# First adaLN rows of layer 0: shifts on TensorE into one PSUM bank, scales as row products on the vector engine, another load order; and another tile order in the first W2 block of an MLP chunk

## The reference

```
sh1, sc1, g1, sh2, sc2, g2 = split(silu(cond) @ mod_w[i] + mod_b[i], 6)
h = rmsnorm(x, norm1_g[i]) * (1 + sc1) + sh1
x = x + g1 * mixer_i(h)              # layer 0: gated short convolution; layer 1: latent attention
h = rmsnorm(x, norm2_g[i]) * (1 + sc2) + sh2
x = x + g2 * (square(relu(h @ mlp_w1[i])) @ mlp_w2[i])      # d_ff = 4096
```

## Time and profile before

| | |
|---|---|
| median of 3 runs | 3317.0 us (3314.32 to 3317.49) |
| profiled execution | 3313.17 us, span 3311.3 us |
| mean granted TensorE clock | 0.954 |
| PE busy | 3070.7 us (93%) |
| DVE busy | 1469.5 us (44%) |
| ACT busy | 1011.1 us (31%) |
| POOL busy | 855.9 us (26%) |
| chain that ended last | PE 61%, issue 23%, DVE 9%, ACT 4%, POOL 2% |

### The profile page before, as it was taken

One profiled execution on the slowest core, in us unless ns is written; L12 is line 12 of the kernel. 1 busy time (PEld: TensorE's weight loads), 2 busy tenths in 40 slices (PEclk: granted clock), 3 DMA queues, 4 the chain that ended last, 5 costly groups with the idle time before them and its releaser, 6 DMA issues.

```text
span 3311.3 us, 43718 instructions
## 1 busy us (share of the span) xinstructions
PE 3070.7 (93%) x17193; PEld 2931.1 (89%) x17193; DVE 1469.5 (44%) x1856; ACT 1011.1 (31%) x1447; POOL 855.9 (26%) x509
## 2 busy tenths in 40 slices
PE   7999998999999999877888888888898999999999
PEld 7999998999999999876777777776798999999999
DVE  2654545555544556554455554564324222222222
ACT  2211113111111112223666667556613111111111
POOL 0122111212212121111553446445421112212121
PEclk6999998999999999886999999899999999999999
DMA  4122220222111221200000000000110111111111
GB/s 192 66 84 94 75 90 32 77 77 82 63 69 64 89 76 63 93 11 7 6 7 2 7 5 7 8 6 0 77 44 26 45 39 44 44 38 39 44 44 76
DMA packets 45532, 166.60 MB, mean 50 GB/s; under 512 B 5792, under 2 KB 7456, under 8 KB 45216
## 3 DMA queue, kind: packets, MB, share of 16 engines
q1 hardware_dynamic: 44912, 160.89, 13.9%
q10 hardware_dynamic: 560, 4.87, 0.4%
HBM read 156.15 MB, written 9.58 MB: 50 GB/s over the span
## 4 chain that ended last, share of the span: by engine, by line
PE 61%; issue 23%; DVE 9%; ACT 4%; POOL 2%; DVEq 0%; ACTq 0%; POOLq 0%
PE ps L822 58%; PE ps L1068 2%; POOL w_lo L459 2%; DVE sums L1586 2%; DVE row_max L1568 1%; ACT p L745 1%; DVE hid_lo L1306 1%; DVE tmp L1301 1%; PE ps L1054 1%; ACT hid_hi L594 1%; ACT tmp L591 1%; DVE q_tok L1543 1%; DVE ssq L1508 0%; DVE k_tok L1548 0%; DVE x L1272 0%
## 5 line engine op out<-in xcount | busy, mean ns | idle before, releaser
L459 POOL TENSOR_TENSOR w_lo<-w_raw,w_hi 128x1024 fp32r<-128x1024 f32 (+2 forms) x190 | 463.4, 2439 | 1979.0 <-ACT w_hi L532 1979.0
L822 PE MATMUL ps<-h_hi,w_hi 128*128 128x384 f32 x2640 | 607.7, 338 | 49.5 <-DVE h_lo L1253 24.6
L822 PE MATMUL ps<-h_lo,w_hi 128*128 128x384 f32 x2640 | 604.2, 336 | 0.0
L822 PE MATMUL ps<-h_hi,w_lo 128*128 128x384 f32 x2640 | 603.1, 336 | 0.0
L822 PEld LDWEIGHTS ps<-h_hi,w_hi 128*128 128x128 f32 x2640 | 474.6, 190 | 54.0 <-issue 43.7
L475 POOL TENSOR_TENSOR p_lo<-p,p_hi 128x512 fp32r<-128x512 f32 (+1 forms) x304 | 384.2, 1273 | 433.8 <-ACT p_hi L747 429.8
L532 ACT ACTIVATE w_hi<-w_raw 128x1024 fp32r<-128x1024 f32 (+2 forms) x190 | 194.6, 1025 | 984.1 <-PE ps L822 912.1
L822 PEld LDWEIGHTS ps<-h_lo,w_hi 128*128 128x128 f32 x2640 | 475.4, 190 | 0.0
L822 PEld LDWEIGHTS ps<-h_hi,w_lo 128*128 128x128 f32 x2640 | 474.2, 189 | 0.0
L1272 DVE SCALAR_TENSOR_TENSOR x<-ps,mod,x 128x256 f32<-128x256 f32 (+5 forms) x432 | 240.1, 611 | 480.0 <-PE ps L822 478.3
L822 PE MATMUL ps<-hid_hi,w_hi 128*128 128x384 f32 x1536 | 350.4, 335 | 9.7 <-DVE hid_lo L1306 9.6
(11 more groups left out here) (135 smaller groups left out, 3587.3 us busy)
## 6 DMA issues: line engine op xcount, KB each, us to landing
w_raw<-in_wall_dram SPq DMA_DIRECT2D x174, 512.0 KB, 3.7
mod_raw<-in_mod_rows_dram SPq DMA_DIRECT2D x80, 512.0 KB, 3.5
mod_first<-in_mod_cols_dram SPq DMA_DIRECT2D x16, 512.0 KB, 15.2
x<-in_x_t_dram SPq DMA_DIRECT2D x8, 576.0 KB, 7.6
x_spill<-x ACTq DMA_DIRECT2D x1, 4608.0 KB, 15.2
x<-x_spill SPq DMA_DIRECT2D x1, 4608.0 KB, 13.7
out_dram<-x SPq DMA_DIRECT2D x8, 576.0 KB, 2.8
w_raw<-in_wall_dram SPq DMA_DIRECT2D x8, 416.0 KB, 3.1
```

The costliest lines, as they stand in the source:

```text
L459: pool.tensor_tensor(w_lo[s][:, 0:words], w_raw[s][:, 0:words], w_hi[s][:, 0:words].bitcast(F32), ALU.subtract).then_inc(w_lo_done, 1)
L822: ins = pe.matmul(out, lhs[a], rhs[b](cols), start=first and n == 0, stop=last and n == 2)
```

## The change

The first eight scales leave TensorE. SP loads their rows of the transposed `mod_w` (`scale_rows`, eight tiles of 512 KB, as many bytes as before) and the DVE makes each as two products against `cond_row` (`first_gain`), and the gain from it in one instruction more. TensorE keeps the eight shifts; they go side by side into 16 columns of bank 6 without a wait between them, three ahead of the sum of squares and five behind it, and one instruction adds all their biases (`shifts_out`). The inverse root stands behind the first two gains in the DVE's queue. ACT squares two tiles ahead of its copy of the condition rows, and makes its first two weight splits ahead of the root. `mod_bias` is loaded ahead of x; the shift tiles are interleaved with x, the first two weight blocks come next, and then scale and remaining shift tiles. In the MLP, the first W2 block of each chunk takes its tiles in an order written out by hand: three of the first half, two of the second, the fourth of the first, and the last two of the second.

```
+FIRST_SHIFTS, FIRST_GAINS = 3, 2
+DOWN_ORDER = [(0, 0), (0, 1), (0, 2), (1, 0), (1, 1), (0, 3), (1, 2), (1, 3)]
...
+        scale_bias = new("scale_bias", [P, KT])
-        mod_first0 = at("mod_first0", [P, KT, WSLOT], F32, G0)
+        mod_shift = at("mod_shift", [P, KT, WSLOT], F32, G0)
+        mod_junk = at("mod_junk", [P, WSLOT], F32, G0 + KT * WSLOT * 4)
-        mod_first1 = at("mod_first1", [P, KT, WSLOT], F32, H0 + KT * N * 4)
+        mod_scale = at("mod_scale", [P, KT, WSLOT], F32, H0 + KT * N * 4 + WSLOT * 4)
+        shift_ps = ps[:, 6 * BANK:6 * BANK + 2 * KT]
...
-            for j in range(KT):
+            sp.dma_start(mod_bias[:, :], T["mod_bias"]).then_inc(const_in, 16)
+            def load_x(j):
                 sp.dma_start(x[:, j, :], T["x_t"][:, j, :]).then_inc(x_loaded[j], 16)
-            sp.dma_start(mod_bias[:, :], T["mod_bias"]).then_inc(const_in, 16)
-            for m in range(FIRST_MODS):
-                tile = (mod_first0, mod_first1)[m // KT]
-                sp.dma_start(tile[:, m % KT, :], T["mod_cols"][m]).then_inc(mf_loaded[m], 16)
+            def load_shift(k):
+                sp.dma_start(mod_shift[:, k, :], T["mod_cols"][k]).then_inc(shift_loaded[k], 16)
+            def load_scale(k):
+                sp.dma_start(mod_scale[:, k, :], T["scale_rows"][k]).then_inc(scale_loaded[k], 16)
+            for j in range(0, KT, 2):
+                load_x(j)
+                load_x(j + 1)
+                load_shift(j // 2)
+            load(0)
+            load(1)
+            for k in range(KT // 2):
+                load_scale(k)
+                load_shift(KT // 2 + k)
+            for k in range(KT // 2, KT):
+                load_scale(k)
-            load_in(0, 0)
+            load_mod(0)
+            load_mod(1)
+            load(2)
+            load_mod(2)
...
-            act.wait_ge(row_mm, 1)
-            act.activation(cond_row[:, :, :].rearrange("p c n -> p (c n)"), ps[:, 0:2 * D], ACT.Copy).then_inc(row_out, 1)
-            rms(x_tile, KT, D)
+            for j in range(KT):
+                if j == 2:
+                    act.wait_ge(row_mm, 1)
+                    act.activation(cond_row[:, :, :].rearrange("p c n -> p (c n)"), ps[:, 0:2 * D],
+                                   ACT.Copy).then_inc(row_out, 1)
+                act.wait_ge(x_loaded[j], 16)
+                square(x[:, j, :], j % 2, D)
             split_hi()
             split_hi()
+            rms(None, 0, D)
+            act.wait_ge(mod_done, FIRST_MODS)
             norm(0, 0, False)
...
-            def first_mod(m):
-                b = 6 + m % 2
-                raw = (mod_first0, mod_first1)[m // KT][:, m % KT, :]
-                pe.wait_ge(mf_loaded[m], 16)
-                if m >= 2:
-                    pe.wait_ge(mod_done, m - 1)
+            def first_shift(k):
+                pe.wait_ge(shift_loaded[k], 16)
+                for j in range(KT):
+                    ins = pe.matmul(shift_ps[:, 2 * k:2 * k + 2], mod_shift[:, k, j * P:(j + 1) * P], cond[:, j, :],
+                                    start=j == 0, stop=j == KT - 1)
                 ins.then_inc(mod_mm, 1)
...
+            def first_down_block():
+                weights()
+                slot = L.at["b"] % 2
+                for half, t in DOWN_ORDER:
+                    if t == 0:
+                        pe.wait_ge(stage_free, L.count("s", 1 - half))
+                    if half == 0:
+                        pe.wait_ge(hid_lo_done, L.count("hid", -t - 1))
+                    v = stage_ps(L.at["s"] + half)
+                    w = t * 2 * P + half * P
+                    ins = three([(v[:, c, :], c) for c in range(3)], t, t == 0, t == HT - 1,
+                                [w_hi[slot][:, w:w + P], w_lo[slot][:, w:w + P]],
+                                [lambda c, h=h: h[:, t, c * TB:(c + 1) * TB] for h in (hid_hi, hid_lo)])
+                    if t == HT - 1:
+                        ins.then_inc(stage_done, 1)
+                L.at["s"] += 2
+                L.at["b"] += 1
...
-            for m in range(KT):
-                first_mod(m)
+            for k in range(FIRST_SHIFTS):
+                first_shift(k)
             pe.wait_ge(row_out, 1)
             sum_squares(KT)
-            for m in range(KT, FIRST_MODS):
-                first_mod(m)
+            for k in range(FIRST_SHIFTS, KT):
+                first_shift(k)
...
+            def shifts_out():
+                dve.wait_ge(mod_mm, KT)
+                dve.tensor_tensor(mod[:, 0:KT, :], shift_ps.rearrange("p (k c) -> p k c", c=2),
+                                  mod_bias[:, 0:KT].unsqueeze(2).to_broadcast([P, KT, 2]), ALU.add).then_inc(mod_done, KT)
+                L.at["m"] += KT
+            def first_gain(k):
+                dve.wait_ge(scale_loaded[k], 16)
+                raw, slot = mod_scale[:, k, :], k % 2
+                for c, product in enumerate((mod_junk[:, :], raw)):
+                    ins = dve.tensor_tensor_reduce(product, raw, cond_row[:, c, :], 1.0, 0.0, ALU.mult, ALU.add,
+                                                   mod_acc[:, slot, c:c + 1])
+                own(ins)
+                g0 = VEC["norm1_g"][0]
+                dve.tensor_scalar(gain[:, 0, k, :], mod_acc[:, slot, :], scale_bias[:, k:k + 1],
+                                  vec[:, g0 + k:g0 + k + 1], ALU.add, ALU.mult).then_inc(mod_done, 1)
+                L.at["m"] += 1
+                dve.wait_ge(mod_done, L.at["m"])
+            def first_norm():
...
+                own(dve.tensor_scalar(scale_bias[:, :], mod_bias[:, KT:2 * KT], 1.0, None, ALU.add))
+                dve.wait_ge(row_out, 1)
+                for k in range(KT):
+                    if k == FIRST_GAINS:
+                        inverse_root(False)
+                    first_gain(k)
+                dve.wait_ge(stage_free, L.at["s"])
+                scaled(0)
+                shifts_out()
+                for k in range(KT):
+                    if k + 1 < KT:
+                        scaled(k + 1)
...
-                first_mod_out(j)
-            inverse_root()
-            for m in range(KT, FIRST_MODS):
-                first_mod_out(m)
-            norm(0, 0, False)
+            first_norm()
```

More of the change, by code:

```diff
@@ L285, in build @@
         m_loaded = [sem(f"m_loaded{s}") for s in range(2)]
-        mf_loaded = [sem(f"mf_loaded{s}") for s in range(FIRST_MODS)]
+        shift_loaded = [sem(f"shift_loaded{k}") for k in range(KT)]
+        scale_loaded = [sem(f"scale_loaded{k}") for k in range(KT)]
         x_loaded = [sem(f"x_loaded{j}") for j in range(KT)]
@@ L930, in chunk @@
                             h_block()
+                    elif k == HT:
+                        first_down_block()
                     else:
@@ L933, in chunk @@
                         for half in range(2):
-                            def hid_ready(t):
-                                pe.wait_ge(hid_lo_done, L.count("hid", -t - 1))
-                            stage(lambda t: t * 2 * P + half * P, HT, (hid_hi, hid_lo),
-                                  hid_ready if k == HT and half == 0 else None)
+                            stage(lambda t: t * 2 * P + half * P, HT, (hid_hi, hid_lo))
                         L.at["b"] += 1
@@ L1174, in own @@
                 dve.wait_ge(dve_self, S.count("n"))
-            def first_mod_out(m):
-                dve.wait_ge(mod_mm, m + 1)
-                dve.tensor_scalar(mod[:, m, :], bank(6 + m % 2, 2), mod_bias[:, m:m + 1], None,
-                                  ALU.add).then_inc(mod_done, 1)
-                L.at["m"] += 1
+            def shifts_out():
[3 more added lines that the diff above has]
+                L.at["m"] += KT
@@ new lines, in first_norm, with scaled @@
+            def first_norm():
+                def scaled(k):
+                    if C["h"]:
+                        dve.wait_ge(h_lo_done, C["h"])
+                    for a, z, c in SEGS:
+                        ins = dve.scalar_tensor_tensor(tmp[k % 2][:, a:z], x[:, k, a:z], gain[:, 0, k, c:c + 1],
+                                                       rstd[:, a:z], ALU.mult, ALU.mult)
+                    ins.then_inc(t_done, 1)
+                    C["t"] += 1
+                own(dve.tensor_scalar(scale_bias[:, :], mod_bias[:, KT:2 * KT], 1.0, None, ALU.add))
[10 more added lines that the diff above has]
+                        scaled(k + 1)
+                    C["h"] += 1
+                    dve.wait_ge(t_done, C["t"] - (1 if k + 1 < KT else 0))
+                    dve.wait_ge(h_hi_done, C["h"])
+                    for a, z, c in SEGS:
+                        ins = dve.scalar_tensor_tensor(h_lo[:, k, a:z], tmp[k % 2][:, a:z],
+                                                       mod[:, k, c:c + 1], h_hi[:, k, a:z].bitcast(F32),
+                                                       ALU.add, ALU.subtract)
+                    ins.then_inc(h_lo_done, 1)
@@ L1214, in add_square, with inverse_root @@
```

(8 more changed lines are left out.)

4 lines of the change are left out of this document (removed).

## The result

The changed kernel took 3271.4 us (median of 4 runs, 3267.2 to 3273.1), the kernel before 3315.7 (median of 4, one run more than in the table above, which gave 3317.0); the ratio is 0.9867 with a 95% interval of 0.9850 to 0.9884. The forecast was 3275, range 3267 to 3288. The profiled execution took 3271.89 us, its span is 3270.1, 41.2 less than before.

The account below looks back on a forecast made before the run. TensorE was taken as the bound, with waits at the start and for hid_lo in each MLP chunk. Savings of 28.2 + 13.9 = 42.1 us took 3313.17 to 3271.1; 3.8 for median over profiled run gave 3275, range 3267 to 3288.

Parts of the forecast that it names:

- without the hold-up everything is 3.1 earlier: Start: bound if GpSimd's weight splits do not slow the DVE's products for the gains; 31.3 us saved.
- six gains, 18.0: Start: the DVE's remaining six gains behind the reciprocal take 18.0 us, ending at 52.5.
- 57.8: Start: forecast time in us of the first layer matmul, 85.97 before, so 28.2 saved.
- So the DVE decides, by about 1.3 us.: End of the start: the DVE's gains, first scaled tile and shift addition end at 54.4, TensorE's five shifts at 52.8.
- with all five shifts at the lower level: Start: bound where TensorE's shifts behind the broadcast all run at 1.2 GHz, end at 55.5 and decide; 26.9 us saved.
- the row behind the old broadcast: Start: earlier profile row with two shifts at the upper clock level (4.02 us) after the same broadcast; basis for 28.2 saved.
- 16 x 0.87: MLP: the wait for hid_lo goes whole in all 16 chunks of both layers, 0.87 us each, 13.9 us.
- The margin of 0.5 us for the residual: W2 blocks, layer 0: the DVE's residual ends at 587.8, TensorE wants that PSUM at 588.4.
- rival (a): W2 blocks: the wait returns as a wait for the residual; 3282 us, or 3289 if layer 1 gains nothing; chance 0.08.
- rival (c): Start: GpSimd does not hold up the DVE's products; 3272 us; chance 0.07.
- Rival (b): Start: saves much less because scale tiles and the reciprocal come late; 3277 to 3289 us, taken as 3285; chance 0.12.
- (d): Behind the start: TensorE stays at the lower clock level; four weight blocks cost 50 us, giving 3325; chance 0.02.

Follow-up runs that it names:

- e5_late_splits: Changed kernel with ScalarE's first two weight splits, and so GpSimd's, moved behind the last gain and shift; one run, 3269.5 us.
- e8_all: Changed kernel with early weight blocks and splits, four shifts ahead, one W2 tile between, additions of squares behind both residuals; median 3263.6 us, ratio to before 0.9857.
- e6_early_weights: Changed kernel with weight blocks 0 and 1 loaded ahead of the last two x tiles and split behind square 5; one run, 3270.9 us.
- e3_one_gain: Changed kernel with the inverse root behind one gain instead of two in the vector engine's queue; two executions, 3273.8 and 3265.1 us.
- e2_w2_only: Kernel before with only the new order of the first W2 block; median 3299.2 us of 8 runs, ratio 0.9958.

## Why the prediction was right, step by step

**The start.** Forecast 28.2 saved, range 26.9 to 31.3; 30.47 in the first profile. The steps up to the mean were right within 0.4: last x tile 20.0 (its square began at 20.19), mean 22.6 (22.92), root 26.9 (26.93). One reading was wrong without effect: the two blocks in 4.45 us did not run at the upper level throughout (it fell near 25.5 us), and a block at that level takes 1.84. That products are held up by the splits was right (e5_late_splits), and gain 0 ended at 30.95 (31.2). But the bound "without the hold-up everything is 3.1 earlier" was wrong: the second scale tile was reckoned to land at 27.7 and came at 29.9 in e5_late_splits, so that only 1.1 was won there. The broadcast began at 33.99 (34.6). Mis-sized was the term "six gains, 18.0": a gain takes 2.74, not 3.0, for the instruction behind the two products starts 0.05 after them and not 0.30 (fixed addresses in straight code are the likely reason, which is only argued). Six took 16.5, which is 1.5 of the 2.3 us by which 57.8 was too late.

**"So the DVE decides, by about 1.3 us."** This step failed. The margin was zero (51.94 against 51.99), so that TensorE's level decides as soon as it is worse. With a start exactly as in the change, the first layer matmul came at 55.5 in two profiles, where about two of the five shifts ran at the upper level, and at 58.5 to 58.7 in three, where none did. The bound "with all five shifts at the lower level" (26.9) is what these three got: 85.97 - 58.6 = 27.4. The 2.3 us by which the first profile beat the forecast therefore contain luck. Here the rule of the Trainium skill (TensorE: Matmul & The Clock Gate, Part 1: The HAM clock gate), by which the level comes back only after sustained work, and the row behind the old broadcast were each right in some executions; neither gives the frequency. The idle time ahead of the broadcast, on which I had set the difference, does not sort the executions. The level came up behind it after 1.4 and 1.8 us of idling (e8_all, e6_early_weights), after 4.4, 5.6 and 7.1 (e3_one_gain, e5_late_splits, the changed kernel), and stayed down after 7.1 in the three. And it had been low long before: in the kernel before it was 0.50 from 26 us on, with TensorE busy, and in the changed kernel from 15 on.

**The W2 blocks.** 0.87 per chunk was right (0.88 in e2_w2_only), and the 0.6 of the list of waits would have been wrong. "16 x 0.87" should have been 15: the last chunk of layer 0 was bound by the vector engine, and the wait for hid_lo in it lay beside a chain that ended later. The margin of 0.5 us for the residual held in the other seven chunks of layer 0; rival (a) came true only in that last chunk, for another reason than the one given, the squares.

**What offset what.** The start won 2.3 more than forecast, the MLPs 2.2 less (one chunk, and 1.4 by the level in layer 1), the stretch between the MLPs, with the attention, took 1.2 more. The sum, 41.2 in the profile against 42.1, is closer than its terms, and that is luck. The forecast of 3275 also carried over the 3.8 us by which the median before lay above its profiled execution; after the change the median (3271.4) lies 0.5 below the profiled one, so that this term did not come true. The measured time is nearest to the 3272 of rival (c), but its mechanism is the one that e5_late_splits rules out. Rival (b) did not come true, but e5_late_splits shows that the transfers were not far from deciding: gain 1 waited 1.35 us for its tile. Rivals (c) and (d) did not come true.

**Left open.** Why the level behind the broadcast comes up in some executions and not in others. The traces show that the five executions with the start of the change part well ahead of it. In the two with 55.5 the level fell to 0.50 near 15 us, and the second shift took 2.0 to 2.1; in the three with 58.6 it fell near 13 us, and the second shift took 3.57. That the execution and not the edit moves this is likely, since the one-gain kernel, the same program twice, had the fall near 14 in one execution and near 15 in the other (shifts 14.33 and 13.96), but no kernel here showed both 55.5 and 58.6. Open too is what sets the time that TensorE spends at the lower level in the attention stretch.

## What to carry to other kernels

Price a wait on a busy engine by the distance between starts of equal work around it, not by its idle time: here 0.87 against 0.6. Before counting a saving once per loop turn, look at the turns that do extra work, for in them another engine may be the bound. Where two chains meet within a few microseconds and one runs on TensorE, work both levels of its clock through. Moving work of the clock-dependent side ahead gives it slack: one shift more ahead of the sum gave it three microseconds in e8_all, of which 0.3 would be left at the lower level, by the estimate there.

## What was unexpected in the hardware

- The hold-up between the vector engine and GpSimd goes both ways. In the changed kernel two splits took 5.64 in place of the 4.66 of e6_early_weights, and the products 1.87 and 3.35 in place of 1.2. The second split (26.22 to 29.50 in the chain that ended last) took 3.28, where one alone takes 2.34, and each product ended 1.1 behind the end of a split, at 27.33 and 30.62.
- It is not confined to row products: two additions of squares took 4.43 instead of 2.80 beside the splits (e6_early_weights), h_lo 3.63 instead of 1.55 (e5_late_splits).
- An unbroken run of two-column matmuls did not hold the upper level. In the changed kernel it was 1.00 from 39 to 42 us, and from 43 to 52 us it was 0.50, with TensorE busy for 8.94 of 9 us and no wait between.
